# Input projections of a two-layer decoder from full float32 to three products of rounded parts, with the rounding work spread over ScalarE, VectorE and GpSimd

## The chip, the core and the metric

The kernel runs on one core of one Trainium2 chip. The metric is device time in microseconds (us) of one launch. TensorE (PE) does the matrix products, VectorE (DVE), ScalarE (ACT) and GpSimd (POOL) the elementwise work, and SyncE (SP) issues nearly all the transfers. Each engine works through its own queue in order, and the queues meet at semaphores.

## What is computed

x is 256 tokens by 1024 features, float32. There are two layers. Each normalises its input, projects it to 2616 columns, gives the columns to four token mixers, projects back and adds; then comes cross-attention to 256 memory tokens, and then a feed-forward part (dense in layer 0, two of eight experts for each token in layer 1).

```
z = rmsnorm(h) @ w_in        # (256,1024) @ (1024,2616), the input projections
a_q,a_k,a_v,a_g,a_lr, b_u, c_q,c_k,c_v,c_qi,c_ki,c_wi, d_uv = split(z)
h += [GLA(a_*) | pool(b_u) | top-64 sparse attention(c_*) | gMLP(d_uv)] @ w_out
h += cross_attention(rmsnorm(h), rmsnorm(mem))
h += swiglu(rmsnorm(h))  (layer 0)   or   top-2-of-8 experts (layer 1)
out = rmsnorm(h)
```

## The kernel before

**Weights.** A ring of seven slots of 128 x 4096 float32 holds the weights of a stage. The input projections of a layer fill it with seven units: QI (the index queries and keys of the sparse attention), A (q, k, v of the linear attention), AG (its gate, 256 columns), CQ (q and k of the sparse attention, 512 columns), CV (256), BU (the pool's input, 256), UV (512). SP issues them in this order. As a unit is used up, SP loads into its slot one of the next stage: WKV (memory keys and values), four parts of W_out (rows 0 to 3), WQ and WO (row 4).

**TensorE.** The normalised, transposed input lies in xnT. `on_features` (L1736) takes a weight tile as the stationary side and 256 tokens as the moving side, eight tiles deep; `on_tokens` (L1741) takes xnT as the stationary side and 256 or 512 weight columns as the moving one. Both are float32 products. The trace has two records for each of them. The order is QI, half of A, the index dot products, the rest of A, AG, CQ (the small logit product stands inside it), CV, the linear attention's 128 x 512 products (L1878), BU, UV. After UV come the small products of the mixers, with the memory keys (128x256 products against memT) among them, and then W_out.

**Rounded parts.** W_out, WO and the dense feed-forward part already use three products. A float32 value v is written as hi + lo, where hi is v in the format fp32r (a copy by ACT) and lo = v - hi, also in fp32r (a subtraction); x w is then hi hi + lo hi + hi lo. `rows_split` makes the parts of W_out: ACT copies 128 x 2048 (L872), POOL subtracts rows 0 and 1 (L732), DVE rows 2 to 4 (L1267).

**VectorE.** While PE works on A and AG, DVE sums the index scores of tokens 128 to 255 and then searches the 64 largest of each row (eight times MAX8 and MATCH_REPLACE8, L1212 and L1213), turns the result into a mask (L1214, L1215), and does the same for tokens 0 to 127 (`score_and_take`). Then come the gates of the linear attention (L1222 to L1230), the copies of q and of cv out of PSUM, and from UV on the layer norm, the logits, the states and the pool's output up to the hi part of the first piece for W_out (L1329).

**GpSimd.** It scales memT (L708, once), scales WKV (L726, eight pieces), makes the lo parts of rows 0 and 1, and then runs the causal pool (L745 to L754), which waits for ACT's copy of BU.

**SyncE.** Its queue is in order: a load whose slot isn't free holds up all that stand behind it.

After the two mixers and the dense part, from about 540 us on, eight or more expert jobs stream 4096-column units of weights through the same ring.

## Time and profile before

| | us |
|---|---|
| median of three runs | 1337.87 (1337.40 to 1337.96) |
| the profiled execution's own time | 1337.72 |
| its span in the profile | 1335.9 |
| PE busy | 1256.2 (94%) |
| DVE busy | 500.4 (37%) |
| ACT busy | 379.0 (28%) |
| POOL busy | 85.1 (6%) |
| moved by DMA | 435.81 MB, mean 326 GB/s |

The span is the time between the first and the last instruction in the trace; about 1.8 us lie around it. Busy shares are of the span. A busy PE is not a PE at its peak: matmuls are pipelined, so the distance from one start to the next is their price, not the duration in the record. All times below count from the start of the span.

### The profile page before, as it was taken

What the parts mean: (1) busy time and instruction counts of PE and PEld (TensorE: products, weight loads), DVE (VectorE), ACT (ScalarE), POOL (GpSimd) and SP (SyncE); (2) the same over time, 40 slices, a digit from 0 to 9 for tenths busy, and PEclk for the clock granted to TensorE, in tenths of its full rate; (3) what the DMA queues carried; (4) which work ended last, traced back from release to release, by engine and by line L of the source; (5) the groups of instructions that cost most, each with busy time, mean ns of one, the idle gap of its engine ahead of it and who ended that gap; (6) DMA issues with size and microseconds to landing.
All of it is one profiled execution on the core that took longest, in us unless ns stands there. A gap on an engine that the chain in (4) does not pass through costs nothing.

```text
span 1335.9 us, 15465 instructions
## 1 busy us (share of the span) xinstructions
PE 1256.2 (94%) x6128; PEld 758.1 (57%) x6128; DVE 500.4 (37%) x886; ACT 379.0 (28%) x603; POOL 85.1 (6%) x69
## 2 busy tenths in 40 slices
PE   8999999999999999999989789889889999999876
PEld 6868888888887787434324224224226888434222
DVE  2736387777653726301001001001006999101002
ACT  2542454444424413101001001001005887101002
POOL 0570000000007300000000000000000000000000
PEclk9999999999999999999999999889889999999999
DMA  9733515442473179799999999999999999899996
GB/s 342 315 126 111 220 54 231 174 163 90 146 294 116 43 276 369 326 428 435 426 434 429 432 429 435 428 432 432 432 432 425 429 427 426 370 428 426 429 429 263
DMA packets 32650, 435.81 MB, mean 326 GB/s; under 512 B 5260, under 2 KB 7376, under 8 KB 9296
## 3 DMA queue, kind: packets, MB, share of 16 engines
q1 hardware_dynamic: 32400, 434.48, 78.4%
q8 instruction: 39, 0.64, 0.2%
q0 software_dynamic: 192, 0.53, 0.1%
q14 instruction: 19, 0.16, 0.0%
HBM read 433.94 MB, written 1.05 MB: 326 GB/s over the span
## 4 chain that ended last, share of the span: by engine, by line
PE 68%; DMA 27%; DVE 2%; ACT 1%; SPq 1%; issue 1%; DVEq 0%
DMA ring<-in_experts 26%; PE bank L2256 14%; PE bank L2349 8%; PE bank L2264 7%; PE bank L1736 7%; PE bank L2133 6%; PE bank L1741 5%; PE bank L1762 4%; PE bank L2137 3%; PE bank L2018 1%; PE bank L2025 1%; PE bank L2019 1%; PE bank L2183 1%; PE bank L2208 1%; DMA ring<-in_packed 1%; ACT r L916 1%
## 5 line engine op out<-in xcount | busy, mean ns | idle before, releaser
L2256 PE MATMUL bank<-ring,xs 128*64 128x512 f32 x1568 | 362.3, 606 | 35.3 <-DMA ring<-in_experts 35.2
L2256 PEld LDWEIGHTS bank<-ring,xs 128*64 128x64 f32 x1568 | 111.0, 139 | 247.9 <-issue 218.2
L1606 DVE TENSOR_TENSOR s_act<-wsT,bank 128x256 f32<-128x256 f32 x49 | 20.6, 421 | 503.4 <-ACT wsT L998 503.4
L2264 PE MATMUL bank<-ring,s_act 128*64 128x512 f32 x736 | 173.7, 612 | 26.6 <-DMA ring<-in_experts 26.5
L2264 PEld LDWEIGHTS bank<-ring,s_act 128*64 128x64 f32 x736 | 53.7, 140 | 132.6 <-issue 120.4
L2133 PE MATMUL bank<-x_both,wf_hi 128*128 128x512 f32 x336 | 118.9, 396 | 0.0
L998 ACT ACTIVATE wsT<-bank 128x256 f32<-128x256 f32 x49 | 18.8, 384 | 331.4 <-PE bank L2208 331.4
L1630 DVE TENSOR_TENSOR w_lo<-ring,w_hi 128x1024 fp32r<-128x1024 f32 x84 | 101.5, 1223 | 12.5 <-ACT w_hi L1056 7.5
L932 ACT ACTIVATE wf_hi<-ring 128x1024 fp32r<-128x1024 f32 x66 | 69.7, 1060 | 96.9 <-PE bank L2133 66.1
L1736 PE MATMUL bank<-xnT,ring 128*128 128x256 f32 (+1 forms) x416 | 94.1, 385 | 2.7 <-DVE xnT L1175 1.1
L1056 ACT ACTIVATE w_hi<-ring 128x1024 fp32r<-128x1024 f32 x84 | 89.0, 1061 | 26.4 <-PE bank L2349 23.6
L2137 PE MATMUL bank<-x_both,wf_lo 128*128 128x256 f32 x336 | 94.2, 280 | 0.0
L1388 DVE TENSOR_TENSOR wf_lo<-ring,wf_hi 128x1024 fp32r<-128x1024 f32 x66 | 80.4, 1222 | 23.1 <-ACT wf_hi L932 23.1
L1736 PEld LDWEIGHTS bank<-xnT,ring 128*128 128x128 f32 (+1 forms) x416 | 77.8, 189 | 16.5 <-issue 3.2
L994 ACT ACTIVATE j_act<-bank 128x512 f32<-128x512 f32 x49 | 29.3, 598 | 188.0 <-PE bank L2256 188.0
L2133 PEld LDWEIGHTS bank<-x_both,wf_hi 128*128 128x128 f32 x336 | 63.1, 188 | 15.0
L1741 PE MATMUL bank<-ring,xnT 128*128 128x256 f32 (+1 forms) x256 | 70.4, 433 | 0.6 <-ACT bias L846 0.6
L2349 PE MATMUL bank<-w_hi,xg 128*128 128x512 f32 x224 | 70.8, 393 | 0.0
L2137 PEld LDWEIGHTS bank<-x_both,wf_lo 128*128 128x128 f32 x336 | 63.4, 189 | 0.9
L1741 PEld LDWEIGHTS bank<-ring,xnT 128*128 128x128 f32 x256 | 48.5, 190 | 20.2 <-issue 15.1
L2208 PEld LDWEIGHTS bank<-cst,j_act 128*128 128x128 f32 x224 | 23.9, 140 | 41.6 <-issue 40.1
L2349 PEld LDWEIGHTS bank<-w_hi,xg 128*128 128x128 f32 x224 | 42.1, 188 | 9.5 <-issue 0.8
(379 smaller groups left out, 1443.9 us busy)
## 6 DMA issues: line engine op xcount, KB each, us to landing
ring<-in_experts SPq DMA_DIRECT2D x93, 2048.0 KB, 20.3
ring<-in_experts SPq DMA_DIRECT2D x36, 4096.0 KB, 25.9
ring<-in_packed SPq DMA_DIRECT2D x18, 1536.0 KB, 6.8
ring<-in_packed SPq DMA_DIRECT2D x11, 2048.0 KB, 13.1
ring<-in_packed SPq DMA_DIRECT2D x18, 1024.0 KB, 5.1
extra<-in_experts SPq DMA_DIRECT2D x3, 2048.0 KB, 9.7
ring<-in_packed SPq DMA_DIRECT2D x2, 656.0 KB, 7.3
ring<-in_packed SPq DMA_DIRECT2D x1, 1312.0 KB, 5.7
```

The source lines that it names most:

```text
L932: act.activation(as_piece(w, ffn_hi(i)), weights, ACT.Copy).then_inc(S["hi_ready"], 1)
L1056: act.activation(w_hi[:, i % NB, 0:hi - lo], ring[:, slot, lo:hi], ACT.Copy)\
L1388: dve.tensor_tensor(as_piece(w, ffn_lo(i)), weights, as_piece(w, ffn_hi(i)), sub)\
L1630: dve.tensor_tensor(w_lo[:, i % NB, 0:hi - lo], ring[:, slot, lo:hi], w_hi[:, i % NB, 0:hi - lo], sub).then_inc(S["lo_ready"], 1)
L1736: i = mm(dst, w[:, k, :], src[:, k, :], start=k == 0, stop=k == KT - 1)
L1741: i = mm(dst, src[:, k, P * t:P * t + P], w[:, k, :], start=k == 0, stop=k == KT - 1)
L1762: ins = mm(dst, x, y, start=opens and n % 3 == 0, stop=closes and n % 3 == 2)
L2133: ins = mm(dst[:, :], wh[:, k, :], x_both[:, k, :], start=k == 0, stop=False, skip_group_check=True)
L2137: ins = mm(dst[:, 0:SEQ], wl[:, k, :], x_both[:, k, 0:SEQ], start=False, stop=k == KT - 1, skip_group_check=True)
L2256: i = mm(ps[d % 2][SMALL * side:SMALL * side + SMALL, :], xs[:, k, :], weights(u)[:, at:at + FC], start=k == 0, stop=k == KT - 1)
L2264: i = mm(ps[6 + half][SMALL * side:SMALL * side + SMALL, :], s_act[:, d % 4, x + side, :], weights(UNIT_OF["out", d, 0])[:, at:at + FC], s ...
L2349: ins = mm(dst[:, :], st_, mv, start=opens, stop=closes)
```

## The change

Five of the seven units of a layer (AG, CV, BU, CQ, UV) are computed as three products of rounded parts; QI and A stay float32. For that:

- ACT copies hi parts: of each unit in pieces of 128 x 2048 (one for AG, CV and BU, two for CQ and UV), and of the input in two halves of 128 x 1024 (x1, tokens 128 to 255, and x0). x_hi lies over buffers that are idle then.
- The lo parts are subtracted by DVE, except AG and CV in layer 0 and the two pieces of CQ in layer 1, which POOL subtracts. The lo parts of the input are made in place, over xnT, once A is done. In layer 1 the hi and lo parts of AG, CV and BU are made while PE is at QI.
- PE's order becomes logit, AG, CV, BU, CQ, the linear attention's products, UV. CV and BU go to other banks. Tokens 128 to 255 of UV come first.
- On DVE the mask after the search moves behind the gates' scan; q's copy moves behind the lo parts of UV and row 2; rows 2 and 3 are subtracted before the linear attention's mask instead of after the first half of UV.
- On POOL memT's scaling moves behind WKV's and is cut in four, and rows 0 and 1 move behind the causal pool and are cut in four pieces each.
- The units get other slots. WKV now takes AG's slot and is loaded once AG is done; the rows of W_out are loaded in the order 2, 3, 0, 1, with 0 behind a wait for CQ and WQ behind one for UV, since hi parts of CQ and UV lie in the slots of QI and A. In layer 1 QI takes a slot that the dense part frees early.
- The mixer's later work, the rest of each layer and the experts are unchanged (a few semaphores are renamed or shared).

The diff, cut to its core:

```diff
-U_A, U_AG, U_CQ, U_CV, U_BU, U_QI, U_UV = SLOTS
-U_WOUT, U_WQ, U_WKV, U_WO = U_A, U_BU, U_QI, U_UV
+U_QI, U_CQ, U_CV, U_BU, U_A, U_AG, U_UV = SLOTS
+U_WOUT, U_WQ, U_WKV, U_WO = SLOTS[0], SLOTS[4], SLOTS[5], SLOTS[6]
+HI_OF = {U_CQ: U_QI, U_UV: U_A}
...
+        assert (uvg_at - kxT_at) % 4 == 0 and kxT_at % 32 == 0
+        x_hi = nc.alloc_sbuf_tensor_at("x_hi", [P, TT, (uvg_at - kxT_at) // 4], F32R, offset=kxT_at, align_bytes=32)
+        x_hi = x_hi[:, :, 0:KT * P].rearrange("p t (k c) -> p t k c", k=KT)
...
+        HI_ORDER = [("ag", "x1", "x0", "cv", "bu", "cq0", "cq1", "uv0", "uv1", "row2", "row3", "row0", "row1", "row4"),
+                    ("ag", "cv", "bu", "cq0", "cq1", "x1", "x0", "uv0", "uv1", "row2", "row3", "row0", "row1", "row4")]
+        LO_POOL = [("ag", "cv", "wkv", "row0", "row1"), ("cq0", "cq1", "wkv", "row0", "row1")]
+        LO_DVE = [("x1", "x0", "bu", "cq0", "cq1", "uv0", "uv1"), ("ag", "cv", "bu", "x1", "x0", "uv0", "uv1")]
+        def hi_count(layer, part):
...
+        def lo_from(layer, part):
+            order, name = (LO_POOL, "lo_done") if part in LO_POOL[layer] else (LO_DVE, "lo_v")
+            return S[name], sum(len(x) for x in order[:layer]) + order[layer].index(part) + 1
...
+            s, at = IN_PARTS[part]
+            return ring_lo[HI_OF[s]][:, at:at + 2048] if s in HI_OF else ring_lo[s][:, 2048:4096]
+        def unit_parts(s):
+            if s in HI_OF:
+                return v3(ring_lo[HI_OF[s]], 0, 4096, KT), v3(ring_lo[s], 0, 4096, KT)
+            return v3(ring_lo[s], 2048, 4096, KT), v3(ring_lo[s], 0, 2048, KT)
+        x_raw = [xnT[:, :, P * t:P * t + P] for t in range(TT)]
+        x_lo = [mix_hi[:, :, P * t:P * t + P] for t in range(TT)]
...
                 unit(1, U_WKV, ring[:, U_WKV, :], packed("wkv", layer))
-                for i in range(4):
+                for i in (2, 3, 0, 1):
+                    if i == 0:
+                        sp.wait_ge(slot_free[U_CQ], turn[1])
                     unit(1, U_WOUT + i, ring[:, U_WOUT + i, 0:2048], packed("wout", layer, i))
+                sp.wait_ge(slot_free[U_UV], turn[1])
                 unit(1, U_WQ, ring[:, U_WQ, 0:2048], packed("wq", layer))
                 unit(1, U_WO, ring[:, U_WO, 0:2048], packed("wo", layer))
                 if layer < 1:
...
-            gp.tensor_tensor(memT[:, :, :], memT[:, :, :], rs_mem.unsqueeze(1).broadcast_to([P, KT, MEM]), ALU.mult)\
-              .then_inc(S["xT_v"], 2)
+            gp.tensor_copy(gmask[:, :], uvg[:, 1, :]).then_inc(S["zeroed"], 1)
...
+                def lo_of(part):
+                    gp.wait_ge(S["hi_done"], hi_count(layer, part))
+                    gp.tensor_tensor(part_lo(part), part_raw(part), part_hi(part), ALU.subtract).then_inc(S["lo_done"], 1)
+                def rows_split(n):
+                    gp.wait_ge(S["hi_done"], hi_count(layer, f"row{n}"))
+                    for c in range(0, 2048, 512):
+                        i = gp.tensor_tensor(row_lo(n)[:, c:c + 512], ring[:, ROWS[n], c:c + 512], row_hi(n)[:, c:c + 512],
+                                             ALU.subtract)
+                    i.then_inc(S["lo_done"], 1)
+                gp.wait_ge(S["scored"], first)
+                take_wait()
+                if layer < 1:
+                    lo_of("ag")
+                    gp.wait_ge(S["scored"], second)
+                    lo_of("cv")
+                else:
+                    lo_of("cq0")
+                    lo_of("cq1")
...
+                if layer < 1:
+                    gp.wait_ge(S["xT_a"], count(0, 2, 2, 2))
+                    for k in range(0, KT, 2):
+                        i = gp.tensor_tensor(memT[:, k:k + 2, :], memT[:, k:k + 2, :],
+                                             rs_mem.unsqueeze(1).broadcast_to([P, 2, MEM]), ALU.mult)
+                    i.then_inc(S["xT_v"], 2)
...
+                take_wait()
+                for n in range(2):
+                    rows_split(n)
...
+                def hi_of(*parts):
+                    for part in parts:
+                        if part[0] == "x":
+                            t = int(part[1])
+                            i = act.activation(x_hi[:, t, :, :], x_raw[t], ACT.Copy)
+                        else:
+                            act.wait_ge(arrived[IN_PARTS[part][0]], layer * (16 * LAYER_TURNS) + 16)
+                            i = act.activation(part_hi(part), part_raw(part), ACT.Copy)
+                        i.then_inc(S["hi_done"], 1)
+                if layer:
+                    hi_of("ag", "cv", "bu")
...
+                if layer < 1:
+                    act.wait_ge(S["zeroed"], 2)
+                    hi_of("ag", "x1")
+                else:
+                    hi_of("cq0", "cq1", "x1", "x0")
...
+                    hi_of("x0")
...
+                if layer < 1:
+                    hi_of("cv", "bu")
+                else:
+                    hi_of("uv0", "uv1")
...
+                if layer < 1:
+                    hi_of("cq0", "cq1")
...
+                if layer < 1:
+                    hi_of("uv0")
...
+                if layer < 1:
+                    hi_of("uv1")
...
+                out_of("bu", bu[:, :, PAD:PAD + SEQ], v3(ps[2], 0, 512, 2))
+                rows_split(2)
+                rows_split(3)
...
+                out_of("uv1", uvg[:, 1, :], ps[7][:, :], ACT.Gelu_apprx_tanh)
+                rows_split(0)
...
+                out_of("uv0", uvg[:, 0, :], ps[4][:, :], ACT.Gelu_apprx_tanh)
...
+                def lo_of(*parts):
+                    for part in parts:
+                        dve.wait_ge(S["hi_done"], hi_count(layer, part))
+                        if part[0] == "x":
+                            t = int(part[1])
+                            i = dve.tensor_tensor(x_lo[t], x_raw[t], x_hi[:, t, :, :], sub)
+                        else:
+                            i = dve.tensor_tensor(part_lo(part), part_raw(part), part_hi(part), sub)
+                        i.then_inc(S["lo_v"], 1)
+                if layer:
+                    lo_of("ag", "cv")
...
+                if layer:
+                    lo_of("bu")
...
+                    factors(layer, 2)
+                take(1, 256)
+                dve.wait_ge(slot_free[U_A], ended[0])
+                lo_of("x1", "x0")
+                sums(0, P)
...
+                take(0, P)
+                if layer < 1:
+                    lo_of("bu")
...
+                chosen(1, 256)
+                chosen(0, P)
+                if layer < 1:
+                    lo_of("cq0", "cq1")
...
+                out_of("cv", cv[:, :, :], v3(ps[3], 0, 512, 2))
+                lo_of("uv0", "uv1")
+                def rows_split(n):
+                    dve.wait_ge(S["hi_done"], hi_count(layer, f"row{n}"))
+                    dve.tensor_tensor(row_lo(n), ring[:, ROWS[n], 0:2048], row_hi(n), sub)
+                dve.wait_ge(g_ev["ag"], L1)
+                for t in range(TT):
+                    link(dve.tensor_tensor(sg[:, t, :], sg[:, t, :], bc[:, 0, :], mult))
+                rows_split(2)
...
+                rows_split(3)
...
+                moments(1)
+                dve.wait_ge(S["bias_done"], 1)
+                group("uv0")
+                bias_and_choice(1, 256)
...
+                def tokens(dst, xs_, w, t, opens=False, closes=False):
+                    for k in range(KT):
+                        i = mm(dst, xs_[:, k, :], w[:, k, :], start=opens and k == 0, stop=closes and k == KT - 1,
+                               skip_group_check=True)
+                    return i
+                def features(dst, w, lo=False, opens=False, closes=False):
+                    for k in range(KT):
+                        if lo:
+                            into, x = dst, mix_hi[:, k, :]
+                        else:
+                            into, x = dst.rearrange("p (t c) -> p t c", t=TT), x_hi[:, :, k, :]
+                        i = mm(into, w[:, k, :], x, start=opens and k == 0, stop=closes and k == KT - 1,
+                               skip_group_check=True)
+                    return i
+                def hi_ready(part):
+                    pe.wait_ge(S["hi_done"], hi_count(layer, part))
+                def lo_ready(part):
+                    pe.wait_ge(*lo_from(layer, part))
+                def side(bank, n):
+                    return ps[bank][:, 256 * n:256 * n + 256]
+                wh, wl = unit_parts(U_AG)
+                hi_ready("ag")
+                for t in (1, 0):
+                    hi_ready(f"x{t}")
+                    tokens(side(5, t), x_hi[:, t, :, :], wh, t, opens=t == 1)
+                    lo_ready("ag")
+                    tokens(side(5, t), x_hi[:, t, :, :], wl, t)
+                for t in (1, 0):
+                    lo_ready(f"x{t}")
+                    i = tokens(side(5, t), x_lo[t], wh, t, closes=True)
+                i.then_inc(g_ps["ag"], 1)
+                wh, wl = unit_parts(U_CV)
+                hi_ready("cv")
+                pe.wait_ge(S["rel"], second)
+                for t in range(TT):
+                    tokens(side(3, t), x_hi[:, t, :, :], wh, t, opens=t == 0)
+                    tokens(side(3, t), x_lo[t], wh, t)
+                lo_ready("cv")
+                for t in range(TT):
+                    i = tokens(side(3, t), x_hi[:, t, :, :], wl, t, closes=True)
+                i.then_inc(g_ps["cv"], 1)
...
+                pe.wait_ge(g_ev["av"], L1)
+                wh, wl = unit_parts(U_CQ)
+                hi_ready("cq1")
+                for m in range(4):
+                    features(side((7, 4)[m // 2], m % 2), wh[:, :, P * m:P * m + P], opens=m % 2 == 0)
+                    features(side((7, 4)[m // 2], m % 2), wh[:, :, P * m:P * m + P], lo=True)
+                lo_ready("cq1")
+                for m in range(4):
+                    i = features(side((7, 4)[m // 2], m % 2), wl[:, :, P * m:P * m + P], closes=True)
+                    if m == 1:
+                        i.then_inc(g_ps["q"], 1)
...
+                pe.wait_ge(g_ev["bu"], L1)
...
+                wh, wl = unit_parts(U_UV)
+                hi_ready("uv1")
+                for t, bank, name in ((1, 7, "q"), (0, 4, "k")):
+                    pe.wait_ge(g_ev[name], L1)
+                    tokens(ps[bank][:, :], x_hi[:, t, :, :], wh, t, opens=True)
+                    tokens(ps[bank][:, :], x_lo[t], wh, t)
+                lo_ready("uv1")
+                for t, bank in ((1, 7), (0, 4)):
+                    i = tokens(ps[bank][:, :], x_hi[:, t, :, :], wl, t, closes=True)
+                    i.then_inc(g_ps[f"uv{t}"], 1)
```

## Rows read from the trace of the kernel before

**Rows 1.** The page: part 4 by line, and the page's row of the experts' products.
```profile
PE 68%; DMA 27%; DVE 2%; ACT 1%; SPq 1%; issue 1%; DVEq 0%
...
L2256 PE MATMUL bank<-ring,xs 128*64 128x512 f32 x1568 | 362.3, 606 | 35.3 <-DMA ring<-in_experts 35.2
```
**Rows 2.** Busy time by stage: stretch, PE, PEld, DVE, ACT, POOL, clock, DMA share, GB/s.
```profile
51.20:95.40 44.20, 44.20 (x170) 31.34 (x168) 17.06 (x38) 18.84 (x22) 35.79 (x26) 1.00 0.36 136
95.40:116.20 20.80, 20.57 (x143) 17.64 (x142) 18.32 (x45) 10.39 (x27) 1.91 (x2) 1.00 0.15 51
...
540.00:1335.90 795.90, 725.18 (x3382) 324.64 (x3378) 173.72 (x221) 169.14 (x259) 0.00 (x0) 0.98 0.98 419
```
**Rows 3.** The chain that ended last, layer 0's projections: start, us, what.
```profile
44.20 7.14 PE bank L1741 x32
...
55.43 10.56 PE bank L1736 x48
65.98 6.91 PE bank L1741 x32
...
81.74 13.73 PE bank L1741 x32
```
**Rows 4.** The same chain, fp32r products of 256 columns in the dense part.
```profile
175.25 3.79 PE bank L2099 x32
```
**Rows 5.** PE's timeline in the dense part, fp32r, 512 and 256 columns in turn.
```profile
200.12 0.39 PE L2133 MATMUL bank<-x_both,wf_hi 128*128 128x512 f32 x1
200.35 0.28 PE L2137 MATMUL bank<-x_both,wf_lo 128*128 128x256 f32 x1
```
**Rows 6.** By source line: hi and lo parts; ns min/median/max, first and last start.
```profile
L872 ACT ACTIVATE ring_lo<-ring x10: 1902/1902/1910, 66.6 to 465.3; 128x2048 fp32r<-128x2048 f32 x10
L732 POOL TENSOR_TENSOR ring_lo<-ring,ring_lo x4: 4510/4514/4519, 69.7 to 425.9; 128x2048 fp32r<-128x2048 f32 x4
L1267 DVE TENSOR_TENSOR ring_lo<-ring,ring_lo x6: 2281/2304/2811, 89.9 to 472.7; 128x2048 fp32r<-128x2048 f32 x6
L1388 DVE TENSOR_TENSOR wf_lo<-ring,wf_hi x66: 1215/1224/1228, 166.2 to 350.6; 128x1024 fp32r<-128x1024 f32 x66
```
**Rows 7.** POOL's timeline of layer 0: beside DVE's searches, and beside DVE's subtractions.
```profile
41.88 4.53 POOL L708 TENSOR_TENSOR memT<-memT,diag 128x2048 f32<-128x2048 f32 x1 [6.92 <-remote]
...
89.37 0.73 POOL L745 TENSOR_TENSOR pw<-pw,cst 64x256 f32<-64x256 f32 x1
90.17 2.66 POOL L747 TENSOR_TENSOR bu<-pw,bu 64x256 f32<-64x256 f32 x1
```
**Rows 8.** DVE's timeline, layer 0: search, score sums, masks, a gate, the tail after UV.
```profile
44.98 0.41 DVE L1213 MATCH_REPLACE8 score<-m,score 128x256 f32<-128x256 f32 x1
...
47.44 2.68 DVE L1203 SCALAR_TENSOR_TENSOR score<-r,wis,score 128x128 f32<-128x128 f32 x7
...
55.90 0.23 DVE L1214 TENSOR_SCALAR score<-score 128x128 f32<-128x128 f32 x1
56.16 0.29 DVE L1215 TENSOR_TENSOR score<-score,cst 128x128 f32<-128x128 f32 x1
...
60.91 0.42 DVE L1224 SCALAR_TENSOR_TENSOR glab<-glab,gla 128x256 f32<-128x256 f32 x1 [3.94 <-ACT gla L858]
...
107.70 0.17 DVE L1261 TENSOR_SCALAR st<-st 128x4 f32<-128x4 f32 x1
```
**Rows 9.** By source line: POOL's WKV pieces begun at 58.4, 59.9 and 405.6.
```profile
L726 POOL TENSOR_SCALAR ring<-ring,columns x2: 1558/1560/1561, 58.4 to 59.9; 128x512 f32<-128x512 f32 x2
...
L726 POOL TENSOR_SCALAR ring<-ring,columns x1: 1567/1567/1567, 405.6 to 405.6; 128x512 f32<-128x512 f32 x1
```
**Rows 10.** DVE's timeline, layer 1, beside POOL's scaling of WKV: a mask.
```profile
405.69 0.69 DVE L1215 TENSOR_TENSOR score<-score,cst 128x128 f32<-128x128 f32 x1
```
**Rows 11.** ACT's timeline, layer 0: the second softmax of the tail begins.
```profile
108.96 0.40 ACT L890 ACTIVATE xnT<-xnT,st 128x128 f32<-128x128 f32 x1
```
**Rows 12.** SyncE's queue after layer 1's mixer: the first loads of the experts.
```profile
470.95 17.54 SPq L645 DMA_DIRECT2D ring<-in_experts  x4
```

134 lines of the change are left out of this document (51 added, 83 removed).

## The prediction

> **What bounds the kernel now.** I read the page's chain first: PE holds 68% of it and DMA 27%, nearly all of the latter in the experts, where PE sat 35 us waiting for weights [rows 1]. The stretches say where: from 540 us on the DMA share is 0.98, between 51 and 95 us it is 0.36 and PE is busy throughout at full clock, with DVE busy 17 of 44 us and ACT 19 [rows 2]. So the projections are PE's own time, and the other engines have room there. The last view, the chain in layer 0, walks from product to product without a gap: AG 7.1, three quarters of CQ 10.6, CV 6.9, UV 13.7 [rows 3]. Layer 1 has the same pattern. After UV the mixer needs 20.8 us up to the first product of W_out [rows 2]; there DVE is the busy engine (18.3 us).
>
> **What PE gives up and takes on.** Before, per layer: AG 7.1, CQ 10.6 x 4/3 = 14.1, CV 6.9, BU as CV 6.9, UV 13.7; together 48.7 us [rows 3]. After: three products for one. AG, CV and BU are 48 fp32r products of 256 columns each, CQ is 96, together 240; UV is 48 of 512. Thirty-two products of 256 columns, each with a new stationary tile, took 3.79 us, so 0.118 us each [rows 4]; one of 512 starts 0.23 us before the next [rows 5]. 240 x 0.118 + 48 x 0.233 = 28.3 + 11.2 = 39.5 us. PE saves 9.2 us a layer, 18.4 in both, if it is always fed.
>
> **What the parts cost the others.** A hi part of 2048 columns takes ACT 1.90 us; per layer seven of these and two halves of x at about 1.06 are 15.4 us. A lo part takes DVE 2.28 to 2.30 us alone (about 2.24 from start to start in a row), half of x 1.22, POOL 4.51 [rows 6]. DVE gets five parts and x, 13.7 us. ACT's copies fit: each stands ahead of its user in the schedule below.
>
> **The port.** DVE and POOL delay each other when both read from SBUF, and this decides the size. A POOL operation of 0.73 us took 2.66 when it began just after a DVE subtraction of 2.30 us [rows 7], and the next DVE subtraction took 2.81 instead of 2.30 [rows 6]: each waited for the other. Beside the search there was no such thing: a search step took its usual 0.41 us while POOL was in a long product [rows 7, 8]. POOL's scaling of WKV (1.57 us a piece) is in between. A DVE operation that began 1.0 us into a piece took its normal 0.42 us [rows 8, 9]; a mask at 405.69 took 0.69 instead of 0.29, beside a piece begun at 405.6 [rows 8 to 10]. So a piece holds the port for about its first 0.5 us, and a long DVE subtraction holds POOL back until it ends. I take 0.5 us for a piece, and for a POOL subtraction its length less 0.2 us (0.73 held the other for 0.51).
>
> **Layer 0, step by step.** I set up the queues in their new order with these durations.
> - DVE ends the search of tokens 128 to 255 at 45.4 [rows 8], subtracts x1 and x0 (2.4), sums the scores of the other tokens (3.1 with its first step [rows 8]) and is at 51.0. POOL may begin CV's lo part only then (it waits for these scores) and ends at 55.5. PE begins the logit product at 44.1, is through AG at 50.4 and through CV's first four groups at 54.1. It waits 1.4 us for POOL.
> - DVE then has the gate's input (0.5), the second search (5.7, from 50.2 to 55.9 before [rows 8]), BU's lo part 2.24, a wait for ACT 0.45, two gate steps 1.1, the two masks 1.2, CQ 4.5, three gate steps 1.5, cv's copy 0.7, UV 4.5, the gate's norm 0.9, row 2 2.24, and only then q's copy 0.7, which frees the bank that UV's first product wants. That is 19.9 us from 57.2, so 77.1; six port waits of 0.45 behind scaling pieces make it 79.8. PE is there at 76.4 and waits 3.4 us.
> - With these, UV ends at 91.1 instead of 95.4. That gain of 4.3 is 9.2 less 1.4 and 3.4 (and 0.1 of rounding).
> - POOL is pushed back by the long subtractions: scaling ends near 77 instead of 69.7 [rows 6], memT near 85, the pool near 96, and rows 0 and 1 run from 96 to 106. PE wants row 0 only at about 115, so POOL itself is hidden with 9 us to spare. But its eight pieces of 1.13 us now lie beside DVE's states and layer norm, where before POOL was idle. Five DVE operations with two SBUF inputs each meet a running piece and wait 0.76 us (1.13 less 0.2 for early release, less 0.17 since the piece began). DVE's work there ran without a gap to 107.87, and ACT's second softmax began at 108.96 [rows 8, 11], so 1.1 us could be covered. But ACT came late there because of the linear attention's output, and that hangs on a state which one of the five waits delays too, so I let nothing be covered: 5 x 0.76 and 0.1 before the first logit, 3.9 us.
> - Layer 0: -9.2 + 1.4 + 3.4 + 3.9 = -0.5 us.
>
> **Layer 1.** BU, CV and AG are split while PE is at QI, when DVE and ACT are idle, and memT isn't scaled again. POOL's second part of CQ runs until 396.9; DVE's subtraction of x1 has to wait for it, and PE waits 1.1 us. q's copy ends at about 423.6 and PE wants it at 424.9: no wait. Rows 0 and 1 are split from 437 to 446.5, mostly beside operations that read PSUM; two DVE operations wait, 1.4 us on the path. -9.2 + 1.1 + 1.4 = -6.7 us.
>
> **The rest.** QI's earlier load in layer 1 gives nothing, since PE is in the dense part until then. WKV is loaded only at 50, when AG is done, lands at about 56 and is scaled in time (in layer 0 the memory keys start at 93, memT is ready at 85). The loads of W_out in the order 2, 3, 0, 1 are queued behind WKV on SP; row 2 lands near 62 and ACT copies it at 70. WQ and WO wait for UV, as WO did, and are wanted 30 us later. The experts' stream starts when W_out frees slots, 6 us after its first product at 465 [rows 12], so it moves with the mixer and a gain passes through.
>
> **Sum.** -0.5 - 6.7 = -7.2 us. The profiled execution took 1337.72 us, span 1335.9; the median is 0.15 above it. 1337.7 - 7.2 = **1330.5 us**.
>
> **The rivals.**
> - *The port costs nothing worth counting.* POOL's pieces slip in between DVE's, for instance because DVE's waits fall where PE has slack. Then layer 0 keeps 9.2 - 1.4 - 0.7 = 7.1 and layer 1 9.2: 1321.4 us. For it speaks that most gate steps in the trace ran undisturbed; against it the 2.66 and the 2.81. Chance 0.2.
> - *A scaling piece holds the port for its whole 1.57 us.* Then each long subtraction of DVE waits up to 1.5 us and POOL's follow; in layer 0 q's copy slips from 80 to about 92, in layer 1 to about 432. By the same queues layer 0 ends 9.8 us later than before and layer 1 0.7 later: 1348 us. It decides from a hold of about 1.0 us on, where the two layers together come out even. The Trainium skill, page "SBUF — State Buffer", section "SBUF: two separate sides", says just this: the one that starts first has the shared pair "for the whole instruction" and the other fully blocks. The trace agrees for POOL's two-input operations against DVE's subtractions (2.66, 2.81), and not for scaling: 0.42 us at 60.91, inside a piece that ran from 59.9 to 61.5 [rows 8, 9]. Chance 0.08.
> - *The weights' load sets the pace.* If an fp32r product of 256 columns cost what a load of its tile shows, 0.19 us, PE would take some 17 us more a layer; part of that fills its waits, so about +20 in all: 1350. 3.79 us for 32 speaks against it [rows 4]. Chance 0.02.
> - *What is gained is given back.* DVE's long queue (20 us between the search and q's copy) or the experts' stream, which hangs on DMA at 0.98, swallows it: a hold of 0.8 to 1.0 us, or three more waits in each tail. Within 0.2% of before, 1337.7. Chance 0.15.
>
> **How the numbers follow.** The forecast has 0.55; its own range goes from -12 to -3 us (no wait in the tails, or one of 1 us more for each long subtraction in layer 0), 1325.7 to 1334.7. The rest stands above. 0.2% is 2.7 us, about what a measurement can tell from no change. Faster takes the forecast and the first rival, 0.75; same 0.15; slower 0.10. The range from 1320.5 to 1338.5 leaves out the two slow cases and the edge of the fast one, some 0.15.
>
> **What would show it.** In the profile after: AG's products of 256 columns 0.118 us apart; PE idle for 1 to 2 us before CV's last third and about 3 us before UV in layer 0, with DVE's q copy named; the same step without a wait in layer 1; L726-like pieces of up to 3.5 us beside DVE's subtractions; several 128x256 DVE operations of about 1.2 us instead of 0.42 after UV in layer 0, few in layer 1; UV's end near 91 and 436, the first product of W_out near 116 and 458; the experts' first load 7 us earlier. It would be wrong if PE waited at a place not named here, if scaling pieces held DVE over 1 us each, or if the experts' start didn't move.

## The result, and the profile after

The changed kernel takes 1341.6 us (median; 1338.4 to 1347.3), the kernel before, on the same chip and in turn with it, 1337.9 (1337.1 to 1340.2): a ratio of 1.0028, with a 95% interval from 1.0018 to 1.0037. It is slower by 0.3%, where 0.5% faster was forecast. The profiled execution took 1339.3 us, its span is 1337.1.

I read four moments out of TensorE's timeline of both kernels, and of one experiment that comes below. "Mixer" is the stretch from the end of UV to the first product of W_out.

| us | before | after | rows 0 and 1 on VectorE |
|---|---|---|---|
| UV ends, layer 0 | 95.4 | 88.7 | 88.8 |
| first product of W_out, layer 0 | 116.25 | 117.85 | 111.48 |
| UV ends, layer 1 | 444.2 | 438.0 | 431.6 |
| first product of W_out, layer 1 | 465.0 | 465.2 | 452.5 |
| span | 1335.9 | 1337.1 | 1323.5 |

So the projections gained 6.7 us in layer 0 and 7.8 in layer 1 (which began 1.6 later), and the two mixers lost 8.3 and 6.4. From the first product of W_out in layer 1 to the end it is 870.9 us before and 871.9 after.

Busy time by stage, after (columns as in [rows 2], which the first two lines answer to; the third answers to its last):
```profile
50.40:88.70 38.30, 36.38 (x248) 32.54 (x247) 29.81 (x49) 23.74 (x26) 36.24 (x21) 1.00 0.46 165
88.70:117.80 29.10, 22.15 (x142) 18.81 (x142) 26.86 (x48) 12.56 (x28) 20.26 (x20) 0.88 0.20 73
540.00:1337.10 797.10, 726.80 (x3382) 326.60 (x3378) 173.95 (x221) 169.04 (x259) 0.00 (x0) 0.98 0.98 418
```
The mixer of 20.8 us has become one of 29.1. TensorE stands idle for 7 of them, GpSimd is busy for 20 where it was for 2, and TensorE's granted clock is 0.88 on average and no longer 1.00: by stretches of 2 us it is 0.50, 1.2 GHz, from about 107.7 to 114.5.

The chain that ended last, layers 1 and 0 (start, us, what); [rows 3] answer to the first two lines:
```profile
399.94 8.07 PE bank L1977 x64
408.01 16.91 PE bank L1988 x144
```
```profile
87.57 3.60 ACT ring_lo L961 x2
...
99.01 1.39 DVE uvg L1412
100.42 1.37 DVE uvg L1413
```
The split products do what was computed for them: 144 in 16.91 us, 0.117 each, without a gap. Behind UV the chain no longer runs on TensorE. It goes over ScalarE's rounding of rows 0 and 1, then over VectorE.

VectorE's timeline in layer 0's mixer, to be held against [rows 8]:
```profile
98.58 0.40 DVE L1410 TENSOR_SCALAR uvg<-uvg,st 128x256 f32<-128x256 f32 x1
99.01 1.38 DVE L1412 TENSOR_TENSOR uvg<-uvg,bc 128x256 f32<-128x256 f32 x1
100.42 1.37 DVE L1413 TENSOR_TENSOR uvg<-uvg,bc 128x256 f32<-128x256 f32 x1
101.72 1.36 DVE L1410 TENSOR_SCALAR uvg<-uvg,st 128x256 f32<-128x256 f32 x1
...
105.81 1.75 DVE L1378 TENSOR_TENSOR xnT<-bias,score 128x512 f32<-128x512 f32 x1
```
And in layer 1, beside the same subtractions of GpSimd:
```profile
443.56 1.22 DVE L1386 TENSOR_REDUCE st<-xnT 128x4 f32<-128x1024 f32 x1
444.81 1.28 DVE L1387 TENSOR_SCALAR st<-st 128x4 f32<-128x4 f32 x1
446.01 1.33 DVE L1401 TENSOR_TENSOR Sst<-bank,cst 128x256 f32<-128x256 f32 x3
447.37 2.84 DVE L1404 SCALAR_TENSOR_TENSOR Sst<-Sst,gla 128x256 f32<-128x256 f32 x2
```
GpSimd beside it (its subtractions of rows 0 and 1 are the last line of each layer; the scaling of WKV, with [rows 9] of before, the first):
```profile
59.25 23.15 POOL L785 TENSOR_SCALAR ring<-ring,columns 128x512 f32<-128x512 f32 x8
82.37 5.05 POOL L790 TENSOR_TENSOR memT<-memT,diag 128x512 f32<-128x512 f32 x4
...
98.78 11.12 POOL L764 TENSOR_TENSOR ring_lo<-ring,ring_lo 128x512 fp32r<-128x512 f32 x8
```
```profile
410.74 20.28 POOL L785 TENSOR_SCALAR ring<-ring,columns 128x512 f32<-128x512 f32 x8
...
442.34 10.27 POOL L764 TENSOR_TENSOR ring_lo<-ring,ring_lo 128x512 fp32r<-128x512 f32 x8
```
An operation of 0.42 us takes 1.37 as soon as rows 0 and 1 are being subtracted, and 0.40 just before (98.58). Not every operation of VectorE waits: a reduction (L1386) and operations with one input in PSUM (L1401) took their usual 1.22 and 1.33 us beside the pieces, while L1387 took 1.28 instead of 0.17 and L1404 2.84 instead of 1.01. GpSimd reaches these rows 3 to 5 us later than computed (96 and 437), because its scaling took 23.2 and 20.3 us.

### The profile page after: what moved, and what is told of

It reads as the page before. It is cut to its first block, busy times and chain, and to the rows that moved or that the text cites. A ratio compares the mean times of both kernels' runs of the same rounds, so it can differ in the third digit from the quotient of the medians.

```text
span 1337.1 us, 15912 instructions
## 1 busy us (share of the span) xinstructions
PE 1243.6 (93%) x6320; PEld 764.7 (57%) x6320; DVE 540.9 (40%) x900; ACT 407.7 (30%) x621; POOL 118.3 (9%) x92
## 3 DMA queue, kind: packets, MB, share of 16 engines
HBM read 433.94 MB, written 1.05 MB: 325 GB/s over the span
## 4 chain that ended last, share of the span: by engine, by line
PE 62%; DMA 27%; DVE 6%; ACT 3%; issue 1%; SPq 1%; DVEq 0%
DMA ring<-in_experts 26%; PE bank L2432 14%; PE bank L2525 8%; PE bank L2440 7%; PE bank L2309 6%; PE bank L1882 4%; PE bank L2313 3%; PE bank L1856 3%; PE bank L1977 2%; PE bank L2194 1%; PE bank L2201 1%; PE bank L2195 1%; PE bank L2359 1%; PE bank L2384 1%; PE bank L1988 1%
## 5 line engine op out<-in xcount | busy, mean ns | idle before, releaser
L1856 PE MATMUL bank<-xnT,ring 128*128 128x256 f32 (+1 forms) x224 | 51.5, 390 | 2.5 <-DVE xnT L1264 1.1
L1856 PEld LDWEIGHTS bank<-xnT,ring 128*128 128x128 f32 (+1 forms) x224 | 41.7, 189 | 10.9 <-DMA ring<-in_packed 2.3
L2525 PE MATMUL bank<-w_lo,xg 128*128 128x512 f32 x112 | 43.6, 390 | 0.0
L785 POOL TENSOR_SCALAR ring<-ring,columns 128x512 f32<-128x512 f32 x16 | 43.4, 2730 | 0.2
```

What stands on the lines that cost most here:

```text
L785: i = gp.tensor_scalar(w, w, pcol[layer][:, R_MEM + k:R_MEM + k + 1], None, ALU.mult)
L1856: i = mm(dst, w[:, k, :], src[:, k, :], start=k == 0, stop=k == KT - 1)
L2525: ins = mm(dst[:, :], st_, mv, start=opens, stop=closes)
```

## The experiments

Theory A: VectorE waits for GpSimd's pieces in the mixers. Theory B: TensorE's clock, which falls to half (1.2 GHz) after TensorE stood idle there, is what costs. Theory C: the order on VectorE (q's copy late) or GpSimd's lateness with memT limits layer 0. All mixers in one table, us in layer 0 and in layer 1, each from its own profile. Beside the experiments the kernel before had medians of 1338.1 to 1339.1, so whole times are best compared by the ratio:

| kernel | layer 0 | layer 1 | whole, median | ratio to before |
|---|---|---|---|---|
| before | 20.85 | 20.85 | 1337.9 | 1 |
| after, two profiles | 29.1, 29.8 | 27.2, 29.0 | 1341.6, 1343.3 | 1.0028, 1.0034 |
| rows written only | 21.8 | 21.6 | 1328.5 | 0.9931 |
| rows on VectorE | 22.7 | 20.85 | 1325.6 | 0.9903 |
| TensorE kept busy | 28.0 | 32.2 | 1345.3 | 1.0054 |
| q's copy first | 25.1 | 21.7 | 1327.1 | 0.9911 |
| pieces of 256 | 28.5 | 29.2 | 1340.8 | 1.0013 |
| rows uncut | 31.4 | 28.7 | 1344.1 | 1.0054 |
| pieces of 256, 20 products | 31.2 | 31.0 | 1345.0 | 1.0044 |
| pieces of 256, 5 products | 25.3 | 25.1 | 1332.9 | 0.9966 |
| scaling left out | 28.7 | 23.4 | 1389.0 | |
| memT early | 20.85 | 20.85 | 1326.7 | 0.9915 |
| memT after CV | 22.2 | 22.2 | 1328.2 | 0.9922 |
| memT on VectorE | 23.5 | 20.8 | 1326.4 | 0.9915 |

### GpSimd writes rows 0 and 1 and reads nothing

```diff
-                        i = gp.tensor_tensor(row_lo(n)[:, c:c + 512], ring[:, ROWS[n], c:c + 512], row_hi(n)[:, c:c + 512],
-                                             ALU.subtract)
+                        link(gp.memset(row_lo(n)[:, c:c + 512].bitcast(F32), 0.0))
+                        i = gp.memset(row_lo(n)[:, c:c + 512].bitcast(F32), 0.0)
```


> The changed kernel, but GpSimd writes zeros into the lo parts of rows 0 and 1 of W_out (two memsets of 512 columns for each subtraction) instead of subtracting, so the products with these two lo parts add nothing. GpSimd has about as much to do at the same place, and reads nothing. Port theory (GpSimd's reads hold VectorE's operations with two SBUF inputs in the tail after UV): the 128x256 operations of the layer norm fall from 1.37 to 0.42 us, the tail from UV's end to the first product of W_out from 29.1 to about 22.5 us in layer 0 and from 27.3 to about 22.5 in layer 1, the clock stays full in it, and the median is 11 to 13 us below the changed kernel's 1341.6, near 1329. Lateness theory (GpSimd is just too late with its queue, whatever it does): no change, 1341. Clock theory (the loss is TensorE's clock falling to half in the tail for reasons of its own): the clock falls at the same places and the time stays above 1338.

It took 1328.5 us, ratio 0.9931 (0.9907 to 0.9956): 13 us less than the changed kernel. GpSimd's and VectorE's timelines in layer 0:
```profile
100.80 0.53 POOL L764 MEMSET ring_lo<- 128x512 f32 x1
101.39 0.65 POOL L765 MEMSET ring_lo<- 128x512 f32 x1
```
```profile
101.62 0.42 DVE L1412 TENSOR_TENSOR uvg<-uvg,bc 128x256 f32<-128x256 f32 x1
102.08 0.42 DVE L1413 TENSOR_TENSOR uvg<-uvg,bc 128x256 f32<-128x256 f32 x1
```
GpSimd is busy in the same place, and VectorE's 128x256 operations with two inputs take 0.42 us; of those with one input (L1410) one took 0.82 in each layer. So what costs is that GpSimd reads, not that it works (A). ScalarE still rounds rows 0 and 1 between uv1's and uv0's output here, and the mixers are 0.9 and 0.8 us longer than before: so at most that much of the loss is ScalarE's, net of what other waits cover. In the profiles the gain is 10.8 us and not 13, since UV in layer 0 ended at 91.9 and not at 88.7: TensorE waited 2.40 us for q's copy, not 1.55, and its clock was at half for 3.4 us in UV.

### Rows 0 and 1 on VectorE, before UV ends

VectorE was idle from 80.7 to 87.6 in layer 0 and from 428 to 436.8 in layer 1. ScalarE rounds both rows ahead of uv1's output, VectorE subtracts them there, GpSimd doesn't.
```diff
+                rows_split(0)
+                rows_split(1)
                 out_of("uv1", uvg[:, 1, :], ps[7][:, :], ACT.Gelu_apprx_tanh)
-                rows_split(0)
-                rows_split(1)
...
                 i.then_inc(S["att_done"], 1)
+                for n in range(2):
+                    dve.wait_ge(S["hi_done"], hi_count(layer, f"row{n}"))
+                    dve.tensor_tensor(row_lo(n), ring[:, ROWS[n], 0:2048], row_hi(n), sub).then_inc(S["lo_v"], 1)
```


> The changed kernel with rows 0 and 1 copied by ScalarE before its copy of UV's first half, and subtracted by VectorE right after the linear attention's mask, in the 7 us (layer 0) and 9 us (layer 1) for which it idles before UV ends. Nothing is left out. Port theory: as in the run with writes only, about 1329; TensorE doesn't wait longer before UV since VectorE is idle there, and UV ends at 88.7 as before. A rival: the rows land too late (they are loaded only after CQ's end at 73.7), ScalarE's copies then hold UV's copy out and VectorE runs into the tail: UV's first copy slips from 87.0 past 88, the tail shrinks less, 1334.

1325.6 us, ratio 0.9903 (0.9882 to 0.9924), the lowest median of all and 1.2% below the changed kernel. It holds the same products on TensorE and the same subtractions; two rows are subtracted some 17 us earlier and by another engine, and ScalarE rounds them ahead of uv1's output and not between uv1's and uv0's. GpSimd's and TensorE's timelines show what is left in layer 0:
```profile
84.46 7.13 POOL L790 TENSOR_TENSOR memT<-memT,diag 128x512 f32<-128x512 f32 x4
```
```profile
91.70 4.55 PE L1856 MATMUL bank<-memT,ring 128*128 128x256 f32 x20 [0.92 <-issue]
```
memT comes late for the memory products. The mixer of layer 1, where there is no memT, is back at 20.85 us.

### TensorE kept busy in the changed kernel

`keep_busy(7, 6)` computes six float32 products of 256 columns into bank 7, and nobody uses the results.

```diff
+                pe.wait_ge(g_ev["kx"], L1)
+                keep_busy(7, 6)
                 pe.wait_ge(S["vn_done"], L1)
...
+                keep_busy(7, 8)
                 pe.wait_ge(S["p"], second)
-                pe.wait_ge(g_ev["kx"], L1)
```


> The changed kernel with 6 and 8 idle products of 256 columns ahead of TensorE's two long waits in the tail (before the gMLP's products and before the second softmax's transposes), into a bank that is free there. Clock theory (half clock after these waits is most of the loss and all of the spread of 9 us between executions): the granted clock stays at 1.00 through the tail, the time falls by 5 us or more, and the executions agree within 3 us. Port theory: the clock stays full, but only what TensorE itself did at half clock comes back, 0.8 us in layer 0 and 1.2 in layer 1, so about 1339.5; the layer norm's operations stay at 1.37 us.

1345.3 us, ratio 1.0054 (1.0032 to 1.0076). In layer 0 the clock stayed at 1.00 and the first product of W_out came 1.05 us earlier (116.80): that is B's share there. In layer 1 TensorE stood idle before the first of these products, as its timeline shows:
```profile
449.34 0.40 PE L2138 MATMUL bank<-zeros,gla 128*64 128x256 f32 x1 [2.62 <-DVE Sst L1404]
...
455.47 3.87 PE L1810 MATMUL bank<-cst 128*128 128x256 f32 x12
```
The clock fell to 0.50 in what followed, at about 451, before the extra products had begun. The six (12 records) took 3.9 us, where they took 2.8 in layer 0, in front of the useful ones. Theory B alone falls: with the clock held, 28.0 us of mixer are left in layer 0.

### q's copy first, and CQ's second lo part late in layer 1

On top of rows on VectorE.
```diff
-                rows_split(2)
                 out_of("q", qT[:, :, :], v3(ps[7], 0, 512, 2))
+                rows_split(2)
                 rows_split(3)
...
                     lo_of("cq0")
+                    gp.wait_ge(S["scored"], second)
                     lo_of("cq1")
```


> As rows_on_dve, and VectorE copies q out before it subtracts row 2, and in layer 1 GpSimd makes the second lo part of CQ only after the second score sums, beside the second search. Queue theory (TensorE waits for what stands ahead on VectorE's queue): the wait of 1.55 us before UV in layer 0 falls to under 0.3, the one of 0.94 us before AG's last third in layer 1 goes, and the time is 2 to 2.5 us below rows_on_dve. Rival: VectorE's later work (row 2, mask, rows 0 and 1) takes up the gap and is late for the tail instead: the same time as rows_on_dve.

1327.1 us, nothing gained. The waits that it aimed at (1.55 us before UV in layer 0, 0.94 in layer 1) are gone, UV ended at 87.3, and layer 1 up to UV's end took 9.1 us less than before, of the sum's 9.2. TensorE's timeline says where it went:
```profile
91.79 8.83 PE L1857 MATMUL bank<-memT,ring 128*128 128x256 f32 x32 [2.47 <-issue]
```
memT was ready at 91.7 whichever way UV went. TensorE waited 2.5 us for it, and then the memory products took 8.83 us instead of 7.17, because the clock fell to half during them. In layer 1 0.8 us came back in the mixer, and 1.5 from there to the end.

### Finer pieces, and whole rows

```diff
-                    for c in range(0, 2048, 512):
+                    for c in range(0, 2048, 256):
```


> The changed kernel, with GpSimd's subtraction of rows 0 and 1 cut into 8 pieces of 256 columns a row instead of 4 of 512; the same work. In the changed kernel seven 128x256 VectorE operations of layer 0's mixer took 1.37 us instead of 0.42, each as long as a piece lasted. If a VectorE operation waits for the end of the piece that is running (hold), each now waits about half as long, 0.8 to 0.9 us for one: the mixer from the end of UV to the first product of W_out becomes 3 us shorter in layer 0 (29.1 to about 26) and 2 us in layer 1 (27.3 to about 25), and the whole some 5 us faster than the changed kernel, about 1336. If the two engines share the port at a lower rate each (sharing), the operations stay at 1.37 us and the time at 1340 to 1342. If the price were that GpSimd is late at all, nothing changes either, or it becomes a little slower by the eight more pieces.

> The changed kernel, with rows 0 and 1 each subtracted by GpSimd in one operation of 2048 columns (4.5 us) instead of four. Hold: one VectorE operation in each of the two stands for up to 4.1 us and no other waits, so two waits of together 6 to 8 us in layer 0 instead of seven of 0.95 (6.7), about the same sum; in layer 1 one or two of them. The whole 1340 to 1345, and in the trace one operation of some 4 us for each row. Sharing: all operations in the stretch are 1.37 us as before.

By source line, the gate's 128x256 product in the two kernels, pieces of 256 first, and VectorE's timeline with whole rows:
```profile
L1412 DVE TENSOR_TENSOR uvg<-uvg,bc x4: 829/832/833, 99.5 to 452.6; 128x256 f32<-128x256 f32 x4
```
```profile
99.52 4.62 DVE L1412 TENSOR_TENSOR uvg<-uvg,bc 128x256 f32<-128x256 f32 x1
104.18 4.60 DVE L1413 TENSOR_TENSOR uvg<-uvg,bc 128x256 f32<-128x256 f32 x1
108.70 0.40 DVE L1410 TENSOR_SCALAR uvg<-uvg,st 128x256 f32<-128x256 f32 x1
```
The same operation takes 0.83, 1.37 or 4.62 us beside pieces of 256, 512 or 2048 columns. It waits 0.41, 0.95 or 4.2 us, which grows as the piece does, and then runs its 0.42: it is held for nearly a whole piece (4.2 of 4.5), and sharing is excluded. VectorE and GpSimd take turns, one operation each.

Whole rows were slower, 1344.1 us. But the finer pieces gave 1340.8, not the 1336 of the expectation. VectorE ended the sum that the second softmax waits for (L1387) 3.1 us earlier in layer 0 (106.8 against 109.9), and the first product of W_out came at 117.7 all the same. The stretch 108 to 118 us, with TensorE busy in 9.5 of 10 us at half clock:
```profile
108.00:118.00 10.00, 9.47 (x41) 9.12 (x42) 7.86 (x23) 2.45 (x6) 3.55 (x6) 0.50 0.00 1
```

### Pieces of 256, with extra products on TensorE

```diff
+                pe.wait_ge(g_ev["kx"], L1)
+                keep_busy(7, 20)
                 pe.wait_ge(S["p"], second)
-                pe.wait_ge(g_ev["kx"], L1)
```


> The run with pieces of 256 columns, and TensorE runs 20 extra products of 256 columns (some 2.2 us at full clock, results unused) where it waited 2.8 us in layer 0 and 2.65 in layer 1 for the second softmax. With the finer pieces VectorE was 2.8 us earlier in layer 0 (its state sum at 108.2 instead of 111.0), but the first product of W_out came no earlier (117.7 against 117.85): the granted clock was 0.50 from about 107 to beyond 117. Clock theory: kept busy through that wait, the clock stays at 1.00, the first product of W_out comes at 113 to 114.5 in layer 0 and 461 to 463.5 in layer 1, and the whole takes 1333 to 1337. Rival: the clock falls elsewhere or is not what holds the mixer; then the time is 1340 to 1342, or more by the products' own time, as in the other run with kept-busy products (1345.3).

1345.0 us. I had taken 0.11 us for such a product; these are not rounded, and 20 took 8.85 us, far beyond the wait. With 5:

> The run with 20 extra products, with 5 of them. There each of the 20 took 0.44 us and not the 0.11 that was assumed: they lasted from 109.3 to 118.0 and outlasted the wait by 5.4 us (ScalarE's softmax was done at 112.6), so the run tells nothing of the sum, but its clock was 1.00 in both mixers. Five take 2.2 us, less than the 2.8 that TensorE waits. Clock theory: the clock stays at 1.00, the mixer from the end of UV to the first product of W_out takes 25 to 26 us in both layers instead of 28.5 and 29.2 with the same pieces and no extra products, and the whole takes 1333 to 1337 instead of 1340.8. Rival: with the clock at 1.00 another engine sets the same end, and nothing changes by over 1 us.

1332.9 us, ratio 0.9966 (0.9954 to 0.9977). By the medians that is 7.9 us less than the same kernel without the five products, by the two ratios 6.3. TensorE's timeline and the same stretch as above:
```profile
105.49 2.38 PE L1810 MATMUL bank<-cst 128*128 128x256 f32 x10
108.46 0.66 PE L2166 MATMUL bank<-cst,xnT 128*128 128x128 f32 x4 [0.59 <-ACT xnT L979]
```
```profile
108.00:118.00 10.00, 8.81 (x55) 7.68 (x56) 9.68 (x26) 4.87 (x9) 3.48 (x6) 1.00 0.00 1
```
2.4 us of work without use in each layer give 3.2 us in layer 0's mixer and 4.1 in layer 1's. Theory B holds where VectorE's waits are shorter and the products end before the wait does.

### The changed kernel once more

> The changed kernel once more, unaltered, for a second profile. Its executions spread over 9 us (1338.4 to 1347.3), while those with rows 0 and 1 on VectorE spread over 0.6. Clock theory: the profiles differ mainly in how long the granted clock stays at 0.50 in the two mixers, so a slower execution shows a longer stretch at 0.50 there and a later first product of W_out (each 2 us of half clock more, about 1 us later); VectorE's and GpSimd's operations are the same to 0.1 us. Rival: the spread arises in the experts, where DMA is at 0.98 to 1.00; then the first product of W_out in layer 1 is at 465.2 in both profiles and the difference lies behind 540 us.

The whole stretch 450 to 464 us in layer 1, the first profile and then the second:
```profile
450.00:464.00 14.00, 11.41 (x77) 9.88 (x77) 13.52 (x33) 4.28 (x13) 2.61 (x2) 0.88 0.01 1
```
```profile
450.00:464.00 14.00, 12.92 (x56) 11.06 (x57) 11.02 (x25) 4.28 (x13) 3.33 (x3) 0.52 0.01 1
```
VectorE's operations up to the second softmax are the same to a tenth, TensorE ran at half clock for 13.5 us instead of 3.4 (by stretches of 2 us), and the first product of W_out came 1.8 us later after UV. So this kernel's time depends on how long the clock stays down after its idle stretches. Both profiles were of executions below the median. Over all 28 executions the mean granted clock was 0.981 to 0.989 in those under 1339 us and 0.971 to 0.975 in those over 1346. That goes with it, but a mean doesn't tell where in the kernel the clock was down, so for the slowest ones this is likely and not shown.

### GpSimd's other work: left out, or elsewhere

Scaling of WKV left out in both layers:
```diff
-                for k in range(KT):
-                    w = ring[:, U_WKV, 512 * k:512 * k + 512]
-                    i = gp.tensor_scalar(w, w, pcol[layer][:, R_MEM + k:R_MEM + k + 1], None, ALU.mult)
-                i.then_inc(S["lo_done"], 1)
+                w = ring[:, U_WKV, 0:8]
+                gp.tensor_scalar(w, w, pcol[layer][:, R_MEM:R_MEM + 1], None, ALU.mult).then_inc(S["lo_done"], 1)
```


> The changed kernel, where GpSimd scales 8 columns of WKV instead of all 4096 (the memory attention's weights stay unscaled; that part is left out). It measures how much of the mixer's loss comes from GpSimd being late: its scaling took 23.2 us in layer 0 and 20.3 in layer 1, where 12.9 and 12.6 were the price before. Without it memT and the pool are done before UV ends, and rows 0 and 1 start when ScalarE has rounded them, near 89 instead of 98.8 in layer 0. Lateness theory: the pieces then lie where VectorE has little to do or reads PSUM, at most three operations wait, and the mixer takes 23 to 24 us in layer 0 and 22 to 23 in layer 1 instead of 29.1 and 27.3: about 1331. If the pieces cost wherever they lie, the mixer still takes 27 us or more in layer 0, and the whole 1337 to 1340.

The whole (1389) can't be compared, since the unscaled memory changes which tokens go to which expert (1120 of the experts' 128x64 products instead of 1568 [rows 1], and three times as many of those of 128x128, L2523); the stages can. Layer 1's mixer took 23.4 us, close to what the lateness theory said. In layer 0 the gain was used up elsewhere: memT and the pool came early, and met VectorE in the projections, as its timeline and TensorE's show.
```profile
60.43 1.41 DVE L1323 TENSOR_TENSOR score<-score,cst 128x256 f32<-128x256 f32 x1
61.87 1.20 DVE L1322 TENSOR_SCALAR score<-score 128x128 f32<-128x128 f32 x1
```
```profile
82.39 3.75 PE L1975 MATMUL bank<-ring_lo,x_hi 128*128 128x512 f32 x8 [6.19 <-DVE qT L1255]
```
UV began 5 us later. And layer 0's mixer took 28.7 us though fewer of VectorE's operations waited there. Its timeline, and one stretch of many with the clock at half:
```profile
102.81 0.85 DVE L1385 TENSOR_SCALAR st<-st 128x4 f32<-128x4 f32 x1
104.93 2.85 DVE L1402 SCALAR_TENSOR_TENSOR Sst<-Sst,gla 128x256 f32<-128x256 f32 x2
107.70 0.40 DVE L1408 TENSOR_SCALAR uvg<-uvg,st 128x256 f32<-128x256 f32 x1
```
```profile
112.00:114.00 2.00, 2.00 (x11) 2.00 (x12) 0.67 (x2) 0.21 (x1) 0.00 (x0) 0.50 0.00 0
```
Rows 0 and 1 began 0.8 us behind UV's end and not 10, three operations waited, 2.5 us together, and VectorE's second state sum ended 16.6 us behind UV's end, where it was 21.2. So for VectorE the lateness theory was right here too. But TensorE, which had waited 2.05 us, ran at 0.50 from about 108 to 122. GpSimd's two-input operations cost wherever they meet VectorE; that they were late in the changed kernel only chose the place.

memT's scaling (four two-input operations) ahead of the score wait, or right behind CV's lo part, or on VectorE, always with rows 0 and 1 on VectorE and q's copy first:

> Rows 0 and 1 on VectorE and q's copy ahead of row 2, as in the last of the runs before, but CQ's second lo part again ahead of the search in layer 1; new: in layer 0 GpSimd scales memT in the 6.7 us that it waits for the scores, ahead of WKV and not behind it. In the run with q's copy first TensorE was through UV at 87.4 and then waited 2.5 us until memT came at 91.7, whichever way UV went, and its clock fell to half during the memory products (8.83 us instead of 7.17). Theory (GpSimd's chain sets layer 0): memory products start at 89 to 90.5 at full clock, the first product of W_out in layer 0 comes at 109.5 to 110.5 instead of 111.5 (rows on VectorE) and 112.4 (q's copy first), and the whole takes 1323 to 1324.5. Rival: memT's four pieces of 1.1 us now delay VectorE's subtractions of x and its score sums, the second search starts 2 us later and all behind it: 1326 to 1328.

> The run with q's copy first (rows 0 and 1 on VectorE, CQ's second lo part late in layer 1), with memT scaled by GpSimd in layer 0 right after CV's lo part, where it otherwise waits for WKV to land and VectorE is in the search, not before it (there it delayed the score sums and CV's lo part, and TensorE waited 3.1 us) and not behind WKV (there the memory products waited 2.5 us and ran at half clock). Theory, GpSimd's place decides: UV ends at 87.4 to 88.5, the memory products start behind it without a wait at full clock, the first product of W_out in layer 0 comes at 108.3 to 109.5 and the whole takes 1322 to 1324. Rival: memT's two-input pieces meet BU's lo part and the gate's steps, each of which then waits up to 1.1 us; BU's or UV's products wait 2 us and nothing is gained over 1325.6.

> The run with q's copy first, with memT in layer 0 scaled by VectorE, in its idle time before UV ends, ahead of rows 0 and 1; GpSimd then does nothing between WKV's scaling and the pool. On GpSimd memT cost in each of three places: behind WKV the memory products waited up to 2.5 us, before and after CV's lo part its pieces held VectorE's subtractions and gate steps. Theory: four products of 512 columns take VectorE 2.7 to 3.5 us from about 81, rows 0 and 1 follow until 88 to 89, the pool's chain on GpSimd ends near 96, the memory products start 2 us behind UV's end (87.4) at full clock, the first product of W_out in layer 0 comes at 108.5 to 110 and the whole takes 1322 to 1324.5. Rival: VectorE is now the late one at UV's end (rows 0 and 1 end 3 us later and the gate's norm with them), and the first product of W_out comes at 111 or later: 1325.5 or more.

1326.7, 1328.2 and 1326.4 us. TensorE's or VectorE's timeline of each:
```profile
57.65 2.80 PE L1976 MATMUL bank<-ring_lo,x_hi 128*128 128x256 f32 x16 [3.13 <-POOL ring_lo L758]
```
```profile
60.64 1.52 DVE L1337 SCALAR_TENSOR_TENSOR glab<-glab,gla 128x256 f32<-128x256 f32 x1
62.19 1.66 DVE L1338 TENSOR_TENSOR_SCAN glab<-cst,glab 128x256 f32<-128x256 f32 x1
```
```profile
80.72 2.90 DVE L1365 TENSOR_TENSOR memT<-memT,diag 128x512 f32<-128x512 f32 x4
83.54 6.17 DVE L1370 TENSOR_TENSOR ring_lo<-ring,ring_lo 128x2048 fp32r<-128x2048 f32 x2
```
Early, memT's pieces held up the subtractions of x and the first score sum, and CV waited 3.1 us; the mixer behind it was back at 20.85. After CV, they held BU's lo part and the gate's steps. On VectorE nothing of this, though the pool's operations now met rows 0 and 1 (6.17 us for the two, where such a pair took 4.5): the first product of W_out in layer 0 came down to 110.5 and layer 1's first product of W_out to 450.2, 2.3 us before that of rows on VectorE, but from there to the end it took 873.1 us instead of 871.0, with the granted clock at 0.95 instead of 0.98 between 700 and 900 us. Why the experts gave that back in this kernel, and in q's copy first (872.5), stays open; the clock alone doesn't tell, since memT early had 0.96 there and took 870.9. No place for memT is measurably better than rows on VectorE alone. So theory C isn't what decides: neither q's copy nor memT's place changed the whole by more than the measurement's own spread.

## Why the prediction was wrong, point by point

- **TensorE's saving, 9.2 us a layer: right.** 0.117 us a product, and 9.1 us in the layer where no wait was left.
- **Waits before UV: right in kind, too high in layer 0.** 0.37 us for GpSimd's lo part of CV (1.4 forecast) and 1.55 for q's copy (3.4 forecast), in the places named. UV ended at 88.7, not 91.1. Layer 1's wait is 0.94 (1.1 forecast).
- **What a scaling piece costs VectorE: right.** One of its short operations after another took 0.83 or 0.70 instead of 0.42 and 0.29. **What it costs GpSimd: too low.** The scaling ended at 82.4, not 77. GpSimd's piece doesn't slip in between two subtractions of VectorE that follow one another: one took 5.2 us, through two of them (4.49 us, from 62.05). The Trainium skill, page "SBUF — State Buffer", section "SBUF: two separate sides", has an exclusive lock that whoever starts first keeps for the whole instruction; GpSimd's two-input pieces and these subtractions agree with it. A scaling piece of 1.57 us that delays VectorE by 0.4 doesn't.
- **The term that failed: the mixers, 3.9 and 1.4 us, measured 8.3 and 6.4.** Following layer 0's chain, 1.8 us are ScalarE, which rounds rows 0 and 1 (3.6 us) between uv1's and uv0's outputs. I costed this edit at nothing and didn't name what is queued behind it. 6.9 us are VectorE's waits from there to its second state sum: six of 0.94 to 1.07 and two of about 0.5, not five of 0.76, since a piece begins as soon as VectorE's operation before has ended, and is waited for nearly in full. 1.5 us of all this is covered, 1.1 of it by the wait for ScalarE that [rows 8, 11] show; I had let nothing be covered. And 1.1 us is TensorE's clock at half, which the text didn't have; it is the 1.05 us that keeping TensorE busy gave back there. In layer 1 the same: 1.75, 4.8, and -0.2 for cover and clock together. There GpSimd came to rows 0 and 1 at 442.3, not at 437, and so met five of VectorE's operations that read SBUF, not two.
- **The rivals.** The one that decided was the fourth, "what is gained is given back ... three more waits in each tail", with 0.15; the number of waits was right, the clock and ScalarE came on top. The full hold of scaling pieces didn't come.
- **The experts' start moves with the mixer: right**, to 1 us in most kernels.
- **A sign of being wrong that it named did come.** TensorE waited at places not named, 2.96 and 3.67 us within layer 0's mixer. And a scaling piece took up to 5.8 us, where 3.5 was the most expected.

## What to carry to other kernels

Before VectorE and GpSimd get work side by side, count one full wait, nearly as long as GpSimd's piece, for each VectorE operation with two inputs in SBUF that runs beside GpSimd operations that read two tensors, and look for idle time of VectorE first. A row that VectorE subtracts in 2.3 us while it has nothing else to do cost less here than the same row on GpSimd, whose own time was free. When an engine's queue gets a step more, price what stands behind it, even if the step itself is off the path. And where a change leaves TensorE idle for some us within a chain that hangs on it, a few products without use, ahead of the wait and done before it ends, can be worth more than a finer cut of the work that it waits for. Too many of them (20), or some behind the idle stretch, lost time here.

## What the runs showed of the hardware

- VectorE and GpSimd took strict turns when both read from SBUF: 0.83, 1.37 and 4.62 us for an operation of 0.42 beside pieces of 0.75, 1.3 and 4.5 us. Even VectorE's one-input operations on 128x256 and 128x4 waited (1.36 and 0.70 us). Its reductions (1.22 us) and operations with an input in PSUM (1.33 us for three) did not.
- GpSimd's writes without reads (0.52 us each) left VectorE's two-input operations at 0.42; a one-input operation of 0.41 took 0.82 once in each layer.
- TensorE's granted clock fell to 0.50, 1.2 GHz, after waits of 2 to 3 us within a mixer, and in the runs with writes only and with memT after CV also after one of 2.4 us before UV. It stayed there for 3 to 14 us, also where TensorE was busy again. It didn't do so every time: after the same wait of 2.64 us in layer 1 (to 450.36 and to 451.08) it stayed at 1.00 in one profile of the changed kernel and was at 0.50 in the other, which came to 3.4 and 13.5 us of half clock. The changed kernel's 18 executions spread over 9 us, the 4 with rows 0 and 1 on VectorE over 0.6; that the clock is the whole of this was not shown.
